# Router product from the residual rows with the root applied to the logits, the best two by largest values and match replacement, and the first gather in four banks, in a one-core decoder layer

## What is computed

```
x = x + cross_attention(rms_norm(x, norm_x), rms_norm(mem, norm_mem), ...)     # ends in o @ w_xo
t = rms_norm(x, norm_moe)
glog = t @ w_rg + b_rg                       # (256, 4)
g_sel, pg = argmax(softmax(glog)), max(softmax(glog))
elog_g = (t @ w_re + b_re)[group g_sel]      # 8 of 32
topv, topi = top_k(softmax(elog_g), 2)
comb[token, expert] = pg * topv / sum(topv)
for e in range(32):
    hid = silu(t @ w_e_gate[e]) * (t @ w_e_up[e])
    out += comb[:, e:e+1] * (hid @ w_e_down[e])
```

## Time and profile before

| | us |
|---|---|
| median of 3 runs | 1034.36 |
| lowest, highest run | 1031.45, 1034.37 |
| profiled execution, its time | 1032.8 |
| its span, first to last instruction | 1031.1 |
| PE busy | 949.9 (92%) |
| DVE, ACT, POOL busy | 450.6, 307.5, 109.0 |

### The profile page before, as it was taken

How to read it: one execution, slowest core, us unless ns; L and a number is a source line. 1 busy time by engine, 2 the same in 40 slices (tenths; PEclk the granted TensorE clock), 3 DMA queues, 4 the chain that set the end, 5 groups by cost and what they waited for, 6 DMA issues and landing times.

```text
span 1031.1 us, 14486 instructions
## 1 busy us (share of the span) xinstructions
PE 949.9 (92%) x5791; PEld 671.8 (65%) x5791; DVE 450.6 (44%) x850; ACT 307.5 (30%) x505; POOL 109.0 (11%) x120
## 2 busy tenths in 40 slices
PE   3999899999999999989889999998989899898995
PEld 3999888898998999779675344444434344443443
DVE  4578996666666765464545121212111121211113
ACT  4455446657557443354340000000000000000002
POOL 2000026845551000000000000000000000000000
PEclk8999899999999999999987999999999899998998
DMA  9455444343235755576273999999999999999991
GB/s 221 135 165 169 136 142 124 123 127 119 83 123 164 205 174 195 169 268 236 89 293 137 424 420 420 421 422 422 422 422 421 422 422 421 422 422 422 421 387 41
DMA packets 110332, 277.72 MB, mean 269 GB/s; under 512 B 14858, under 2 KB 78386, under 8 KB 85706
## 3 DMA queue, kind: packets, MB, share of 16 engines
q1 hardware_dynamic: 110138, 276.50, 71.1%
q10 hardware_dynamic: 144, 0.52, 0.1%
HBM read 275.96 MB, written 1.05 MB: 269 GB/s over the span
## 4 chain that ended last, share of the span: by engine, by line
PE 62%; DVE 12%; DMA 12%; issue 6%; POOL 4%; ACT 3%; SPq 1%; DVEq 0%; POOLq 0%; ACTq 0%
PE bank L1799 17%; DMA up_b<-in_w_e_up_dram 12%; PE bank L1442 8%; PE bank L1444 8%; PE bank L1443 8%; PE bank L1829 8%; DVE lo_w L910 4%; PE bank L1787 4%; POOL work L566 3%; PE bank L1816 2%; ACT hi_w L592 2%; DVE work L1059 2%; DVE work L1060 1%; POOL ysT L554 1%; PE bank L1720 1%
## 5 line engine op out<-in xcount | busy, mean ns | idle before, releaser
L1442 PE MATMUL bank<-u_hi,hi_w 128*128 128x256 f32 x624 | 185.0, 297 | 6.2 <-DVE lo_w L910 6.2
L1444 PE MATMUL bank<-u_hi,lo_w 128*128 128x256 f32 x624 | 178.8, 286 | 0.0
L910 DVE TENSOR_TENSOR lo_w<-raw_w,hi_w 128x2048 fp32r<-128x2048 f32 x68 | 154.8, 2281 | 54.9 <-ACT hi_w L592 54.7
L1443 PE MATMUL bank<-u_lo,hi_w 128*128 128x256 f32 x560 | 160.7, 287 | 0.0
L1799 PE MATMUL bank<-up_a,xg 128*64 128x512 f32 x256 | 122.1, 630 | 19.2 <-DMA up_b<-in_w_e_up_dram 19.2
L592 ACT ACTIVATE hi_w<-raw_w 128x2048 fp32r<-128x2048 f32 x68 | 128.4, 1889 | 32.1 <-PE bank L1444 29.1
L1442 PEld LDWEIGHTS bank<-u_hi,hi_w 128*128 128x128 f32 x624 | 122.1, 196 | 9.7 <-issue 8.9
L1829 PE MATMUL bank<-down_a,moe_buf 128*64 128x512 f32 x256 | 115.0, 601 | 9.5 <-DVE xg L1378 7.6
L1799 PE MATMUL bank<-up_b,xg 128*64 128x512 f32 x256 | 122.3, 631 | 0.0
L1444 PEld LDWEIGHTS bank<-u_hi,lo_w 128*128 128x128 f32 x624 | 121.8, 195 | 0.0
L869 ACT ACTIVATE y_pair_hi<-bank 128x512 fp32r<-128x512 f32 x32 | 17.4, 595 | 338.8 <-PE bank L1829 338.8
(11 more groups left out here) (317 smaller groups left out, 1786.8 us busy)
## 6 DMA issues: line engine op xcount, KB each, us to landing
raw_w<-in_w_in_dram SPq DMA_DIRECT2D x34, 1024.0 KB, 5.5
up_b<-in_w_e_up_dram SPq DMA_DIRECT2D x32, 1024.0 KB, 23.2
up_a<-in_w_e_up_dram SPq DMA_DIRECT2D x32, 1024.0 KB, 21.1
down_a<-in_w_e_down_dram SPq DMA_DIRECT2D x32, 1024.0 KB, 17.4
down_b<-in_w_e_down_dram SPq DMA_DIRECT2D x32, 1024.0 KB, 19.5
gate_a<-in_w_e_gate_dram SPq DMA_DIRECT2D x16, 1024.0 KB, 19.2
gate_b<-in_w_e_gate_dram SPq DMA_DIRECT2D x16, 1024.0 KB, 21.2
gate_c<-in_w_e_gate_dram SPq DMA_DIRECT2D x16, 1024.0 KB, 20.5
```

The costliest lines, as they stand in the source:

```text
L910: tt(lo_w[:, m % RING, 0:w], raw_w[:, m % RING, 0:w], hi_w[:, m % HI_RING, 0:w].bitcast(F32), ALU.subtract).then_inc(lo_done, 1)
L1442: mm(dst, left[0], right[0], start=first, stop=False)
L1443: mm(dst, left[0], right[1], start=False, stop=False)
L1444: return mm(dst, left[1], right[0], start=False, stop=last)
```

## The change

The router weights get the gain once, at the start: one more small load puts `norm_moe` into eight rows of `prow`, the transpose that turns `prow` has 48 rows instead of 40, and DVE multiplies `wr` by it (L973 of the changed kernel). PE then turns the residual rows `xres` themselves, the left half between units xo10 and xo11, and the root multiplies the logits (L1327) instead of the rows. `xn2` is gone: ACT rounds `xres` with the root as scale, DVE's `rows_lo` is one scalar_tensor_tensor. The two experts come from `max` (eight largest) and `match_replace`; the ramp `rev32` is dropped. The slot positions and the selection come before the combine weights, `rows_lo(0)` stands before them and `rows_lo(1)` behind them. Slot numbers start at 1, which drops a subtraction. The first gather runs all high parts over banks 2 to 5 and then all low parts; the counts for later passes move behind it. gate_d's load also waits for `xn_lo_done`.

```diff
+                          (prow[40:48, :], norm_moe[0, :].rearrange("(t p) -> t p", p=P)),
...
             sp.wait_ge(residual_in, 1)
+            sp.wait_ge(xn_lo_done, NT)
             load_expert(GATE[1] + 1, 3, w_e_gate)
...
-                act.wait_ge(xn_ready, 7 + i)
-                nc.scalar.activation(xn_hi[:, i, :, :], xn2[:, i, :].rearrange("p (c k) -> p k c", k=KT), ACT.Copy)\
-                    .then_inc(xn_hi_done, 1)
+                act.wait_ge(rstd_done, 5 + i)
+                nc.scalar.activation(xn_hi[:, i, :, :], xres[:, i, :].rearrange("p (c k) -> p k c", k=KT), ACT.Copy,
+                                     scale=st[:, 14 + i:15 + i]).then_inc(xn_hi_done, 1)
...
-            nc.scalar.activation(rt[:, 96:98], rt[:, 96:98], ACT.Exp).then_inc(rexp_done, 1)
+            nc.scalar.activation(rt[:, 256:320], rt[:, 256:320], ACT.Exp).then_inc(rexp_done, 1)
...
+            def rows_turned(c, i):
+
+                g = group[0]
+                dve.wait_ge(tr_ready, g + 1)
+                nc.vector.tensor_copy(tT[:, 4 * c:4 * c + 4, P * i:P * i + P],
+                                      bank[2 + g % 2][:, :].rearrange("p (k t) -> p k t", k=4)).then_inc(tr_evac, 1)
+                group[0] += 1
...
+            tt(wr[:, :, :], wr[:, :, :], bank[4][:, 136:144].unsqueeze(2).to_broadcast([P, KT, 36]), ALU.mult)\
+                .then_inc(prm_ready, 1)
...
+            split_lo_through(UN["xo00"] + 2)
+            residual_add("xo", 0, 0)
+            residual_add("xo", 0, 1)
+            for i in range(NT):
+                rows_turned(0, i)
+            residual_add("xo", 1, 0)
+            inverse_mean_of_rows(3, 0)
+            residual_add("xo", 1, 1)
+            for i in range(NT):
+                rows_turned(1, i)
+            inverse_mean_of_rows(3, 1)
...
-                tt(xn_lo[:, i, :, :], xn2[:, i, :].rearrange("p (c k) -> p k c", k=KT), xn_hi[:, i, :, :].bitcast(F32),
-                   ALU.subtract).then_inc(xn_lo_done, 1)
...
+                stt(xn_lo[:, i, :, :], xres[:, i, :].rearrange("p (c k) -> p k c", k=KT), st[:, 14 + i:15 + i],
+                    xn_hi[:, i, :, :].bitcast(F32), ALU.mult, ALU.subtract).then_inc(xn_lo_done, 1)
...
+            link(nc.vector.memset(first2, TAKEN))
+            for i in range(NT):
+                dve.wait_ge(rl_ready, i + 1)
+                dve.wait_ge(rstd_done, 5 + i)
+                last = stt(L[:, i, :], bank[4 + i][:, 0:36], st[:, 14 + i:15 + i], brt, ALU.mult, ALU.add)
+            link(last)
...
+            glog = L[:, :, 0:4]
+            link(nc.vector.tensor_reduce(out=gmx, in_=glog, axis=AXX, op=ALU.max))
+            link(tt(oh_g, glog, over(gmx, GROUPS), ALU.is_equal))
+            link(tt(oh_g, oh_g, rev4.unsqueeze(1).to_broadcast([P, NT, GROUPS]), ALU.mult))
+            link(nc.vector.tensor_reduce(out=tmp2, in_=oh_g, axis=AXX, op=ALU.max))
+            link(tt(oh_g, oh_g, over(tmp2, GROUPS), ALU.is_equal))
+            link(ts_(pen, oh_g, -1.0, -NEG, ALU.add, ALU.mult))
             link(tt(em.rearrange("p i (g e) -> p i g e", g=GROUPS),
                     L[:, :, 4:36].rearrange("p i (g e) -> p i g e", g=GROUPS),
-                    oh2[:, :, 0:4].unsqueeze(3).to_broadcast([P, NT, GROUPS, PER_GROUP]), ALU.add))
+                    pen.unsqueeze(3).to_broadcast([P, NT, GROUPS, PER_GROUP]), ALU.add))
...
+            for i in range(NT):
+                last = nc.vector.max(out=top8[:, i, :], in_=em[:, i, :])
+            link(last)
+            link(nc.vector.tensor_copy(first2[:, :, 0:2], top8[:, :, 0:2]))
+            for i in range(NT):
+                last = nc.vector.match_replace(out=em_left[:, i, :], in_to_replace=first2[:, i, :], in_values=em[:, i, :],
+                                               imm_value=TAKEN)
+            link(last)
+            ts_(msk, em_left, TAKEN, None, ALU.is_equal).then_inc(rmask, 1)
+            tt(ge, glog, over(gmx, GROUPS), ALU.subtract).then_inc(rexp_in, 1)
+            tt(e_exp, em, top8[:, :, 0:1].to_broadcast([P, NT, EXPERTS]), ALU.subtract).then_inc(rexp_in, 1)
+            rows_lo(0)
+
+            dve.wait_ge(rmask, 1)
+            dve.wait_ge(rpos, 1)
+            link(tt(pos_all[:, :, 0:EXPERTS], bank[5][:, 0:64].rearrange("p (i n) -> p i n", i=NT), msk, ALU.mult))
+            select(0)
+            nc.vector.tensor_reduce(out=most, in_=bank[5][:, 64:96], axis=AXX, op=ALU.max).then_inc(counts_read, 1)
+            rows_lo(1)
...
+            link(nc.vector.tensor_reduce(out=tmp2, in_=ge, axis=AXX, op=ALU.add))
+            link(tt(cmb, e_exp, msk, ALU.mult))
+            link(nc.vector.tensor_reduce(out=sum2, in_=cmb, axis=AXX, op=ALU.add))
+            link(tt(scale2, sum2, tmp2, ALU.mult))
+            link(nc.vector.reciprocal(scale2, scale2))
+            link(tt(cmb, cmb, over(scale2, EXPERTS), ALU.mult))
...
+            last.then_inc(comb_ready, 1)
...
+            def rows_turned(c, i):
+                g = group[0]
+                wait_evac(pe, f"xo{c}{i}")
+                pe.wait_ge(tr_evac, g - 1)
+                for k in range(4):
+                    last = tp(bank[2 + g % 2][:, P * k:P * k + P], xres[:, i, 512 * c + P * k:512 * c + P * k + P], ident[:, :])
+                last.then_inc(tr_ready, 1)
+                group[0] += 1
...
+            def router_logits(c, i):
+                pe.wait_ge(tr_evac, 13 + 2 * c + i)
+                for k in range(4 * c, 4 * c + 4):
+                    last = mm(bank[4 + i][:, 0:36], tT[:, k, P * i:P * i + P], wr[:, k, :], start=(k == 0), stop=(k == KT - 1))
+                if c == 1:
+                    last.then_inc(rl_ready, 1)
+            tm_steps("xo", 0, a_parts, xo_lo, (4, 8))
+            tm_steps("xo", 1, a_parts, xo_lo, (4, 8), between=lambda: [rows_turned(0, i) for i in range(NT)])
             pe.wait_ge(xexp_done, 8)
             for i in range(NT):
-                transposes_of(xn2, i, split=False)
-                pe.wait_ge(tr_evac, 14 + 2 * i)
-                for k in range(KT):
-                    last = mm(bank[4][:, 36 * i:36 * i + 36], tT[:, k, P * i:P * i + P], wr[:, k, :],
-                              start=(k == 0), stop=(k == KT - 1))
-            last.then_inc(rl_ready, 1)
-
-            wait_evac(pe, "xo11")
+                rows_turned(1, i)
+            for c in range(2):
+                for i in range(NT):
+                    router_logits(c, i)
...
+            def first_gather():
+                pe.wait_ge(m_sel, 1)
+                pe.wait_ge(xn_hi_done, NT)
+                for part in (xn_hi, xn_lo):
+                    if part is xn_lo:
+                        pe.wait_ge(xn_lo_done, NT)
+                    for q in range(4):
+                        if part is xn_hi and q == 3:
+                            pe.wait_ge(counts_read, 1)
+                        for k in (2 * q, 2 * q + 1):
+                            for i in range(NT):
+                                last = mm(bank[2 + q][:, 256 * (k % 2):256 * (k % 2) + 256], part[:, i, k, :], S[:, i, :, :],
+                                          start=(part is xn_hi and k % 2 == 0 and i == 0),
+                                          stop=(part is xn_lo and k % 2 == 1 and i == NT - 1), skip_group_check=True)
+                        if part is xn_lo:
+                            last.then_inc(m_gath, 1)
...
+                if first:
+                    pe.wait_ge(comb_ready, 1)
+                else:
                     pe.wait_ge(m_yhi, 2 * n)
```

More of the change, by code:

```diff
@@ new lines, in later_passes @@
+            def later_passes():
+                for k in range(1, MAX_PASSES):
+                    ts_(pos_all[:, :, EXPERTS * k:EXPERTS * k + EXPERTS], pos_all[:, :, 0:EXPERTS], -1.0 * CAP * k, None,
+                        ALU.add)
+                nc.vector.memset(pos_all[:, :, MAX_PASSES * EXPERTS:], -1000.0)
+                dve.wait_ge(counts_read, 1)
+                link(ts_(passes, most, CAP + 0.5, 1.0, ALU.is_gt, ALU.add))
+                for k in range(2, MAX_PASSES):
+                    link(stt(passes, most, CAP * k + 0.5, passes, ALU.is_gt, ALU.add))
+                ts_(n_it[:, 0:1], passes, float(PAIRS), None, ALU.mult)
+                ts_(n_it[:, 2:3], passes, float(PAIRS // 2), None, ALU.mult)
+                nc.vector.tensor_copy(n_it[:, 1:2], passes).then_inc(route_ready, 1)
@@ L1478, in fm_step, with tm_steps @@
                 last.then_inc(proj_ready, 1)
[L1480 removed]
+            def tm_steps(prefix, c, act_parts, sem=None, halves=None, between=None):
                 banks = {}
@@ L1487, in tm_steps @@
                         pe.wait_ge(sem, halves[half])
+                    if half == 1 and between is not None:
+                        between()
                     for i in range(NT):
```

145 lines of the change are left out of this document (40 added, 105 removed).

## The result

The changed kernel takes **1023.66 us** (median of four, 1022.45 to 1026.23) against 1034.2 for the kernel before beside it: ratio 0.9915, 95% interval 0.9900 to 0.9929. Three further measurements of the same program gave ratios of 0.9921 (0.9906 to 0.9937), 0.9923 (0.9907 to 0.9939) and 0.9934 (0.9919 to 0.9950). Over all 22 executions the median is 1025.25 (1022.45 to 1028.92), against 1032.98 over 68 of the kernel before.

The account below looks back on a forecast made before the run. The expert-weight stream, started by the first gate layer, was taken to bound the end. That layer 3.9 us earlier, minus 0.1 at the program's start, gave 3.8 us off 1033.6: 1029.8 us, range 1026.0 to 1033.0.

Parts of the forecast that it names:

- T0: Start of PE's first gate layer, 559.59 us before the change; moving it was to move the end by as much.
- Steps 1 and 2: PE's sixteen transposes: eight before xo11 cost 1.12 us, so xo11 ends at 533.65; the other eight end about 535.0.
- step 10: Start of the program: one more small load and the `wr` multiplication cost 0 to 0.45 us, 0.1 taken.
- Step 3: Router products on PE: eight instructions at 0.12 us until 536.0, 24 at 0.215; logits at 541.2 against 544.2.
- step 5: PE's residual blocks behind the logits: 5.4 us at 1.2 GHz, hiding the choice of experts; counts at 547.8.
- Step 4: Choice of experts on DVE: 3.1 us with MAX8 and MATCH_REPLACE8 at 0.2 each, against 4.7; mask at 544.3.
- Step 6: `rows_lo(0)` fills DVE to 546.8 beside PE's residual blocks; positions at 547.85, 4.0 us earlier.
- Step 7: Positions to the first gate layer: 7.8 us set by DVE, before 7.75; gate layer starts at 555.65, 3.9 us earlier.
- Steps 8 and 9: `later_passes` (about 1.5 us on DVE) beside the gate layer, and gate_d's load waiting for `rows_lo(1)`: no effect.
- A: Rival: PE's clock stays at 2.4 GHz, first gate layer at 552.3; gain 7.3 us, time 1026.3; chance 0.2.
- B: Rival: DVE later than priced, `rows_lo` at twice 2.065 us; gain only 0.8 us, time 1032.8; chance 0.2.
- C: Rival: slow clock in first expert pair breaks the stream, deciding beyond about 7 us lost; 9 us slower, 1043; chance 0.05.

## Why the prediction was wrong

**The bound.** Right in the main: the stream has no hole, and the first reload is 3.87 us behind T0 at full clock. Too short in one point: the end follows the reload, and between T0 and the reload lies a gate layer whose clock can fall (5.57).

**Steps 1 and 2.** xo11 ended at 533.62 (forecast 533.65), the transposes at 535.05 (535.0). The first agreement is luck: the eight transposes between xo10 and xo11 took 0.79 us from start to next start, not 1.12, and everything behind the start of the program came 0.39 us later, not 0.1 (step 10).

**Step 3 is the one that failed**, and step 5 with it: "I take the fall at 536.0 and a recovery after as much dense work as before, since the pauses and small products that preceded the fall are still there." The products took 3.66 us and the logits stood at 538.6, not 541.2; the residual blocks took 2.82 us, in the changed kernel's profiles with a short fall 4.46 and 4.52, not the 5.4 of the forecast. The small products are indeed still there, but the pauses of 0.60, 0.94 and 0.78 us are not: one of 0.35 is left. My own step 2 had said that the first two are gone; the sentence on the clock contradicts it, and the sum went by the sentence. With two of the pauses filled by dense blocks the kernel before has no fall at 536 either. Whether the closed pauses did it or the denser mixture stays open, and the small shapes are not cleared: in eight of thirteen profiles of the changed order a fall comes at the end of the products, in the third of the changed kernel with no idle PE for 3.9 us before it. What the order decides is when it comes and what it meets: at the residual blocks it lasts 3.4 us; at 536 it met products and pauses and lasted 13.6.

**Step 4.** Logits to mask 2.9 us (3.1). Two MAX8 took 0.29 us together and each MATCH_REPLACE8 0.18, inside my bounds of 0.15 and 0.285; the load of its values, 0.09, I had not listed. But its worth was misjudged through step 5: "no price of MAX8 within its bounds shows". Going back to the twelve steps costs 1.8 us of T0.

**Step 6.** Positions at 543.78 instead of 547.85; the four microseconds of products and blocks again. `rows_lo(0)` fills the gap as said.

**Step 7.** 7.46 us against 7.8, evictions 2.48 for 2.6 and weights 1.8 for 1.85. The order on DVE and the four banks, which I took for free, were worth about 0.55 and 1.05.

**Steps 8 and 9.** Hidden: later passes from 551.11 to 552.26 beside the gate layer; gate_d asked for at 547.12, and the DMA idle again before the reload.

**Step 10.** 0.39 us against 0.1; the upper bound of 0.45 was near. The argument that PE uses the first `lo_w` soon after its end should have led there.

**The rule against.** `rows_lo` as scalar_tensor_tensor took 2.07 and 2.22 us against 2.065; the halved throughput did not come, also not at 1024 columns with a stride.

**The rivals.** A is what happened, and its working holds: 552.3 against 551.24, of which 0.3 lies in the mask, 0.4 between the mask and the positions (2.1 us instead of 2.5) and 0.3 in step 7. Its chance of 0.2 was too low. The argument for it (shorter pauses) fits what the runs show, though they do not prove it; the argument against, that small products did not bring the clock back, says nothing on whether the clock falls while it is up. B did not occur. C's mechanism did, in four profiles (two of them of the changed kernel), but for 3.4 us and 1.7 us of time, far from its point of decision.

## What to carry to other kernels

Before taking a fall of PE's clock as given, list the pauses of PE in front of it and ask which of them the change removes; here the clock that stayed up was worth about as much as all the work that the change removed (8.35 us in all, 3.9 by the forecast that kept the fall). Work without a dependence, such as residual blocks, can be what makes a fall short while another engine decides (3.4 us instead of 13.6): moving it into earlier pauses gave back what the earlier logits had won. And where the clock can fall by chance, compare several profiles before a microsecond is put down to an edit.

## What the runs showed of the hardware

- 2.4 GHz was granted through 16 transposes and all 32 product instructions of 36 columns in eleven profiles: in ten of them eight of the transposes lie behind xo11, with one idle stretch of 0.35 us; in the one with the left half late all sixteen do, with one of 0.60 us. The Trainium skill (TensorE: Matmul & The Clock Gate, "Part 4: PE-mode transpose") says that full rate does not engage for transposes, as they do not count as busy in the same way; here the clock was at 2.4 GHz while they ran.
- Seven falls that began within 0.6 us of the first dense residual block ended after 3.4 us; the one that began 1.2 us before the end of the products lasted 6.8 (added pause), and those with small products or idle PE behind them 13.6 (before, and before with two pauses filled).
- Whatever the program, a fall of the clock in the 440s came in six of sixteen profiles and moved the rest by about 2 us.
